# Stage boundaries of a two-block transformer kernel: column halves of the second tokens, GpSimd for first splits and first layer norms, chunk halves for a stage's first two tiles

## The reference

```
for layer in (0, 1):                                   # first block
    h = modulate(rmsnorm(x)); y = mlstm(h) if layer == 0 else stick_breaking(h, k_sh, v_sh)
    x = x + g1 * y
    h = modulate(rmsnorm(x)); x = x + g2 * peer_ffn(h) # 128*128 experts, top 16 of 8 heads
for l in (0, 1):                                       # second block
    mix = diff_moba(x) if l == 0 else gla(x)
    x = layer_norm(alpha * x + mix)
    x = layer_norm(alpha * x + relu(x @ w1)**2 @ w2)   # width 4096
```

## Time and profile before

| | |
|---|---|
| median of three runs | 2693.94 us (2690.03, 2693.94, 2698.76) |
| the profiled execution, span from first to last instruction | 2688.2 us |
| TensorE matmul busy | 2605.5 us, 97% |
| VectorE, ScalarE, GpSimd busy | 1996.2 (74%), 1506.0 (56%), 346.1 us (13%) |
| mean granted clock of TensorE | 0.995 |

### The profile page before, as it was taken

How to read it: one execution, slowest core, us unless ns; L and a number is a source line. 1 busy time by engine, 2 the same in 40 slices (tenths; PEclk the granted TensorE clock), 3 DMA queues, 4 the chain that set the end, 5 groups by cost and what they waited for, 6 DMA issues and landing times.

```text
span 2688.2 us, 48883 instructions
## 1 busy us (share of the span) xinstructions
PE 2605.5 (97%) x17304; PEld 2387.0 (89%) x17304; DVE 1996.2 (74%) x3791; ACT 1506.0 (56%) x2602; POOL 346.1 (13%) x190
## 2 busy tenths in 40 slices
PE   6999999999999999999999999999999999998998
PEld 6779999999888888889999999888888889887997
DVE  6768957888887876669867888666666686677766
ACT  4455557766565556555557766665554544463443
POOL 4007600000000002617500000000000101002000
PEclk9999999999999999999999999999999999999999
DMA  6844564444788874424664444555555345442553
GB/s 243 282 137 164 197 228 149 142 143 148 266 279 272 280 264 145 149 94 167 204 213 143 148 142 150 195 191 192 195 187 187 108 176 188 165 164 96 187 188 133
DMA packets 134733, 490.88 MB, mean 183 GB/s; under 512 B 15520, under 2 KB 15608, under 8 KB 134288
## 3 DMA queue, kind: packets, MB, share of 16 engines
q1 hardware_dynamic: 131904, 480.31, 52.6%
q0 software_dynamic: 2640, 8.02, 0.9%
HBM read 487.21 MB, written 1.06 MB: 182 GB/s over the span
## 4 chain that ended last, share of the span: by engine, by line
PE 87%; DVE 6%; ACT 2%; DMA 2%; issue 1%; POOL 0%; SPq 0%; DVEq 0%; ACTq 0%
PE ps L224 78%; PE ps L1308 4%; DMA weight_ring<-in_stream 2%; ACT weight_split L239 1%; PE ps L641 1%; DVE weight_split L248 1%; DVE arena L633 1%; ACT arena L396 1%; PE ps L2473 1%; PE ps L1280 1%; POOL weight_split L248 0%; DVE arena L1909 0%; PE ps L389 0%; DVE arena L1913 0%; PE ps L662 0%
## 5 line engine op out<-in xcount | busy, mean ns | idle before, releaser
L224 PE MATMUL ps<-hT_split,weight_split 128*128 128x256 f32 x9792 | 1234.3, 285 | 9.8 <-DVE hT_split L421 4.6
L224 PEld LDWEIGHTS ps<-hT_split,weight_split 128*128 128x128 f32 x9792 | 1196.2, 192 | 20.1 <-issue 13.8
L248 DVE TENSOR_TENSOR weight_split<-weight_ring,weight_split 128x1024 fp32r<-128x1024 f32 x674 | 823.5, 1223 | 403.0 <-ACT weight_split L239 400.4
L239 ACT ACTIVATE weight_split<-weight_ring 128x1024 fp32r<-128x1024 f32 x800 | 848.2, 1061 | 259.7 <-PE ps L224 167.8
L224 PE MATMUL ps<-weight_split,hidden_split 128*128 128x512 f32 x3948 | 914.8, 391 | 7.6 <-DVE hidden_split L1574 4.0
L224 PEld LDWEIGHTS ps<-weight_split,hidden_split 128*128 128x128 f32 x3948 | 736.4, 188 | 160.9 <-issue 8.0
L248 POOL TENSOR_TENSOR weight_split<-weight_ring,weight_split 128x1024 fp32r<-128x1024 f32 x126 | 306.2, 2433 | 410.5 <-ACT weight_split L239 410.2
L1404 ACT ACTIVATE hidden_split<-arena 128x256 fp32r<-128x256 f32 (+1 forms) x256 | 176.3, 689 | 249.0 <-PE ps L224 248.5
L1396 ACT ACTIVATE arena<-ps 128x256 f32<-128x256 f32 (+18 forms) x248 | 126.9, 512 | 133.5 <-PE ps L224 133.5
L224 PE MATMUL ps<-weight_split,hT_split 128*128 128x512 f32 x660 | 159.1, 396 | 9.0 <-DVE weight_split L248 4.7
L1574 DVE TENSOR_TENSOR hidden_split<-arena,hidden_split 128x256 fp32r<-128x256 f32 x256 | 161.2, 630 | 0.0
(11 more groups left out here) (357 smaller groups left out, 1765.7 us busy)
## 6 DMA issues: line engine op xcount, KB each, us to landing
weight_ring<-in_stream SPq DMA_DIRECT2D x912, 512.0 KB, 3.3
x<-in_x SPq DMA_DIRECT2D x1, 1024.0 KB, 5.0
arena<-mlstm_m_rows POOLq DMA_DIRECT2D x1, 1024.0 KB, 6.7
arena<-in_ln_mix_g POOLq DMA_DIRECT2D x2, 512.0 KB, 4.8
arena<-in_ln_mix_b POOLq DMA_DIRECT2D x2, 512.0 KB, 6.2
arena<-in_ln_ffn_g POOLq DMA_DIRECT2D x2, 512.0 KB, 4.6
arena<-in_ln_ffn_b POOLq DMA_DIRECT2D x2, 512.0 KB, 6.3
out<-x SPq DMA_DIRECT2D x2, 512.0 KB, 2.6
```

Of the source, the lines that this page charges most:

```text
L224: mm = pe.matmul(out_, stationary(s_part), moving(m_part), start=start and n == 0, stop=stop and n == 2, skip_group_check=True)
L239: act.activation(wsplit[:, n % SPLITS, HIGH, :], ring[:, slot(POS[n]), :], ACT.Copy).then_inc(high_ready, 1)
L248: eng.tensor_tensor(w[:, REST, :], ring[:, slot(POS[n]), :], w[:, HIGH, :].bitcast(fp32), ALU.subtract).then_inc(split_ready, 1)
```

## The change

- **Second tokens by column halves.** A stage's tail runs the held-back matmuls of tb = 1 for columns 0 to 511 first (`third_done`), then for 512 to 1023. Residual, squares, scaling and the layer norm's sum and statistics are done by these halves; transposes g = 2 and g = 3 wait for a half each. `dense_pe` now holds back three tiles instead of two.
- **GpSimd.** The rests of the first two tiles of peer 0, stick breaking, peer 1, mlp0, gla and mlp1, the high of the second tile of the three rms stages, the rest of hy's first tile, and the unit rows of the first tokens (two instructions of 512 columns) of the three layer norms move to GpSimd. The parameter DMAs that followed on GpSimd now stand behind them.
- **Turn.** The chunks 0 to 3 of the second tokens are split on VectorE as two pieces of 2 chunks (5 parts instead of 4); TensorE starts when the first piece is there.
- **First two tiles by chunk halves.** `two_lin_cols`: chunks 0 to 3 of tile 0, then of tile 1, then chunks 4 to 7 of each.
- **Small.** The epsilon goes into the root's bias; `HOLDS` gets other numbers; tile 1 of an mlp uses bank 3.

```diff
-        HOLDS = {1: (28, 2, 4, 14, 2), 2: (28, 5, 4, 14, 0), 4: (28, 5, 4, 14, 0), 6: (0, 1, 26, 14, 1),
-                 7: (0, 7, 26, 14, 0), 8: (0, 6, 26, 14, 0)}
+        HOLDS = {1: (14, 2, 2, 12, 2), 2: (14, 5, 2, 12, 0), 4: (14, 5, 2, 12, 0), 6: (0, 1, 8, 10, 1),
+                 7: (0, 7, 8, 10, 0), 8: (0, 6, 8, 10, 0)}
...
+SPLIT_WAITS = {True: {0: 2, 2: 3, 4: 4, 6: 5}, False: {0: 2, 4: 3, 6: 4}}
...
+        def two_lin_cols(n, dsts, turn):
+            for chunks in (range(4), range(4, 8)):
+                for k, dst in enumerate(dsts):
+                    if chunks[0] == 0:
+                        pe.wait_ge(split_ready, n + k + 1)
+                    w = wsplit[:, (n + k) % SPLITS]
+                    for c in chunks:
+                        if k == 0:
+                            chunk_split(turn, c)
+                        mm = passes(dst, lambda part: w[:, part, c * 128:(c + 1) * 128], lambda part: hTsplit[:, part, c, :], c == 0, c == 7)
+                    if chunks[0]:
+                        mm.then_inc(tiles_used, 1)
...
+        def norm_turn_dve(n, normed):
+            part_split_dve(n, 1, lambda v: half_of(v, 0), normed)
             for m in range(2):
+                part_split_dve(n, 2 + m, lambda v: v[:, 2 * m:2 * m + 2, 128:T], normed)
+            for m in range(2):
+                part_split_dve(n, 4 + m, lambda v: pair_of(v, m), normed)
...
+            def gated_sum(tb, columns, done):
+                y = ps[:, bank + 2 * tb:bank + 2 * tb + 2, :].rearrange("p a b -> p (a b)")
+                after_dve(dve.tensor_tensor(tok[:, tb, columns], y[:, columns], gate[:, columns], ALU.mult))
+                dve.tensor_tensor(x[:, tb, columns], x[:, tb, columns], tok[:, tb, columns], ALU.add).then_inc(done, 1)
...
-            splits_until(dve, n0)
-            rest(dve, n0)
-            rows_done(k, 1, done_tiles)
-            after_dve(gated_dve(1, gate, bank))
+            gated_sum(0, slice(0, D), x_half)
+            dve.wait_ge(third_done, k + 1)
+            gated_sum(1, slice(0, 512), x_third)
+            dve.wait_ge(tiles_used, done_tiles)
+            gated_sum(1, slice(512, D), x_ready)
             if rms is not None:
+                rms_bias_dve(rms)
                 rms_tok_dve(rms, 0)
                 rms_tok_dve(rms, 1)
...
+        def layer_norm_dve(k, done_tiles, bank=0):
+            dve.wait_ge(half_done, 4 + k + 1)
+            after_dve(ln_sum_dve(0, slice(0, D), bank))
+            after_dve(ln_half_stats_dve(0, 0), ln_half_stats_dve(0, 1))
+            ln_var_dve(0)
+            dve.wait_ge(third_done, 4 + k + 1)
+            after_dve(ln_sum_dve(1, slice(0, 512), bank))
+            ln_rstd_dve(k, 0).then_inc(ln_rstd, 1)
+            ln_half_stats_dve(1, 0)
+            dve.wait_ge(tiles_used, done_tiles)
+            after_dve(ln_sum_dve(1, slice(512, D), bank))
+            after_dve(ln_half_stats_dve(1, 1))
+            ln_var_dve(1)
+            after_dve(ln_rstd_dve(k, 1))
+            ln_unit(dve, 1, 0).then_inc(unit_third, 1)
+            ln_unit(dve, 1, 1).then_inc(x_ready, 1)
+
+        def layer_norm_pool(k, n0):
+            pool.wait_ge(ln_rstd, k + 1)
+            ln_unit(pool, 0, 0).then_inc(unit_first, 1)
+            ln_unit(pool, 0, 1).then_inc(x_half, 1)
+            splits_until(pool, n0)
+            rest(pool, n0)
+            rest(pool, n0 + 1)
...
+        def first_rests_pool(n0):
+            splits_until(pool, n0)
+            rest(pool, n0)
+            pool.wait_ge(tiles_used, n0 + 1 - SPLITS + 1)
+            pool.wait_ge(tile_full[slot(POS[n0 + 1])], full(POS[n0 + 1]))
+            pool.tensor_copy(wsplit[:, (n0 + 1) % SPLITS, HIGH, :], ring[:, slot(POS[n0 + 1]), :]).then_inc(high_ready, 1)
+            rest(pool, n0 + 1)
...
+            down(*first, 0, False, False, 0)
+            down(*second, 0, False, False, 0)
+            down(*third, 0, False, True, 0).then_inc(half_done, 1)
+            down(*first, 0, False, False, 1)
+            down(*second, 0, False, False, 1, (0,))
+            down(*third, 0, False, True, 1, (0,)).then_inc(third_done, 1)
+            down(*second, 0, False, False, 1, (1,))
+            down(*third, 0, False, True, 1, (1,))
...
         def peer_pool(l):
+            first_rests_pool(FIRST[f"peer{l}q"])
             pool.wait_ge(x_ready, 2 * l + 1)
             pool.dma_start(pr_sk, io["sub_keys"][l]).then_inc(pr_par, 16)
...
         def hy_params_pool():
+            splits_until(pool, HY_T)
+            rest(pool, HY_T)
```

More of the change, by code:

```diff
@@ L257, in chunk_split, with tile @@
         def chunk_split(turn, c):
-            if turn is not None and c in (0, 4, 6):
-                pe.wait_ge(x_split_ready, 4 * SPLIT_TURNS.index(turn) + {0: 2, 4: 3, 6: 4}[c])
+            if turn is not None:
+                waits = SPLIT_WAITS[OUT_PARTS[turn] == 5]
+                if c in waits:
+                    pe.wait_ge(x_split_ready, SPLIT_BASE[turn] + waits[c])
         def lin_rows(n0, bank, turn=None, tail=False, split=None, split0=0, between=None, rows_of=lambda part, c: hTsplit[:, part, c, :]):
-            def tile(c, tb):
+            def tile(c, tb, halves=(0, 1)):
                 if tb in (None, 0):
@@ L268, in tile @@
                 for b in range(TB) if tb is None else (tb,):
-                    for half in range(2):
+                    for half in halves:
                         mm = passes(ps[:, bank + 2 * b + half, :], lambda part: rows_of(part, c)[:, b * 128:(b + 1) * 128],
@@ L287, in lin_rows @@
                 mm.then_inc(half_done, 1)
-                for c in range(8 - SPLITS, 8):
-                    tile(c, 1).then_inc(tiles_used, 1)
+                tile(5, 1).then_inc(tiles_used, 1)
+                tile(6, 1, (0,))
+                tile(7, 1, (0,)).then_inc(third_done, 1)
+                tile(6, 1, (1,)).then_inc(tiles_used, 1)
+                tile(7, 1, (1,)).then_inc(tiles_used, 1)
         def lin_cols(n, dst, i=0, step=1, turn=None, moving=hTsplit):
@@ L697, in down @@
                 for b in range(TB) if tb is None else (tb,):
-                    for half in range(2):
+                    for half in halves:
                         mm = passes(ps[:, 2 * b + half, :], lambda part: hidden[:, j % 3, part, b * 128:(b + 1) * 128],
                                     lambda part: w[:, part, half * 512:(half + 1) * 512], start, stop)
-                if tb != 0:
+                if tb != 0 and 1 in halves:
                     mm.then_inc(tiles_used, 1)
@@ L1072, in mlstm_dve @@
                 if a == 3:
-                    for tb in range(TB):
-                        rms_var_dve(0, tb)
                     rms_tok_dve(0, 0)
```

304 lines of the change are left out of this document (151 added, 153 removed).

## The result

The changed kernel took 2703.95 us, the median of six runs (2700.89 to 2704.5); the kernel before, over six runs, 2690.34 us (2686.84 to 2698.76). The ratio is 1.0046, 95% interval 1.0033 to 1.0060: slower, by 9 to 16 us. The forecast time, 2700.9 us, was 3 us from it, partly by luck: the sum of the parts was +7.0 us and the measured difference is +12.4 by the ratio (0.0046 x 2690.34). The three runs from which I started had 2693.94 as their median; the three later ones (2686.84 to 2690.65) lay lower, and this made up for part of the sum's error.

A forecast was written before the change was run, and what follows sets the result against it. TensorE was 87% of the chain that ended last, so the change works on seven boundaries and the end. Terms 6.0 + 0.8 + 1.4 - 0.9 + 0.4 - 0.65 = +7.0 us on 2693.9 gave 2700.9 us, range 2680 to 2710.

The forecast's parts named there:

- three rms boundaries and the stages behind them: Peer 0, stick breaking, peer 1: held VectorE +1.45, early splits -0.38, clock +0.9 each; +6.0 us for three.
- mlp0: Layer-norm boundary: start +0.25, early splits -0.38, clock +0.9; +0.8 us.
- gla, from mlp0's tail to its first products: Layer-norm boundary: start, gate weight's rest, longer tail, late chunks and clock; +1.4 us.
- mlp1: Layer-norm boundary: VectorE late as before, shorter chain shows, -0.7 - 0.38 + 0.2 for the clock; -0.9 us.
- hy: Boundary where only the first tile's rest moves: its add is held like peer 0's, without a copy; +0.4 us.
- end, without mlp1's first products: Kernel's end: three held-back tiles gain 1.4 us, 0.6 to 0.75 lost waiting for the last hidden rest; -0.65 us.
- Taking turns: VectorE and GpSimd at the boundaries wait for each other's whole instructions; the forecast itself, 72%, 2694 to 2709 us.
- the clock's part: TensorE's clock falls after over 4 us without work at rms boundaries; 0.9 us each, bounds 0 and 2.3.
- The overlap rival: GpSimd's instructions do not hold VectorE's at the boundaries: -17 us, 2677 us; 18%.
- Dear GpSimd: One-input GpSimd instructions (copy, unit rows) cost what two-input ones do: +7, 2708 us; 10%.
- Chunk halves and end: Early splits save 0.38 us between a stage's first two tiles; three held-back tiles at the end give -0.65 us.

The follow-up runs named there:

- more_holds: The changed kernel with 44 instead of 14 identity transposes ahead of the turn at the three rms boundaries: 2698.5 us, ratio 1.0023.
- no_gpsimd_work: The changed kernel with all of its new GpSimd work undone, halves kept: 2682.99 us, ratio 0.9974 to the kernel before.
- units_back: The changed kernel with only the layer norms' unit rows of the first tokens back on VectorE: 2699.31 us, ratio 1.0029.
- before_two_rests_gpsimd: The kernel before, with GpSimd making the rests of the first two tiles at the three rms boundaries: 2696.27 us, ratio 1.0026.
- hy_rest_back: The changed kernel with only the rest of hy's first tile back on VectorE: 2698.92 us, ratio 1.0022.
- norm_rests_back: The changed kernel with the first two tiles' rests of mlp0, gla and mlp1 back on VectorE, unit rows still on GpSimd: 2699.29 us, ratio 1.003.

## Why the prediction was right or wrong

| term | predicted | measured in the trace |
|---|---|---|
| three rms boundaries and the stages behind them | +6.0 | +6.3 - 0.9 = +5.4 |
| mlp0 | +0.8 | +1.73 - 0.33 = +1.4 |
| gla, from mlp0's tail to its first products | +1.4 | +0.95 + 0.36 + 0.69 = +2.0 |
| mlp1 | -0.9 | +0.68 - 0.32 = +0.4 |
| hy | +0.4 | +0.33 + 2.65 + 1.56 = +4.5 |
| end, without mlp1's first products | -0.65 | -0.73 + 0.32 = -0.4 |
| mLSTM, no edit of the boundary yet | 0 | +0.92 |

- **Taking turns: right in kind and place at the rms boundaries.** The hold of the third quarter's add and of the scaling, the clock below 1 and a start 10.5 to 11.3 us behind the last row product (forecast: 10 and the clock's part) came as put down; the order of turns was the forecast one at all three boundaries. The start, predicted at 194.2 + 0.9 in before's clock, came at 196.18 - 0.92 = 195.26. In sizes: the hold is +1.0 (more_holds) where I had +1.45, the clock +0.7 to +1.8 where I had 0.9. The Trainium skill (SBUF — State Buffer, "Who interferes with whom") says which VectorE instructions are held, and the trace agrees for GpSimd's rests: adds and scalings held (2.12 instead of 0.69, 2.78 instead of 0.88 us), the product from PSUM not.
- **The overlap rival: refuted** as a behaviour, but its arithmetic was that of another kernel. It gave -1.8 to -2.4 a boundary if nothing were held; no_gpsimd_work has 2.05, 1.05 and 2.05 us less than before, because GpSimd makes no split there that could hold VectorE; at stick breaking the parameter work still does.
- **Dear GpSimd: half right, and only for the unit rows.** The copy took 1.50 in all 15 cases of five traces, but each time it began 0.6 us before the held add ended, so no run shows what it takes alone: from the add's end on it is 0.90, and my 1.2 lies between the two. The unit rows took 2.07, outside my bounds of 0.5 and 1.2: I had bounded an operation with no row by a two-input one of the same engine, as if inputs set its time. At mlp1 this is 0.9 us (units_back) of the 1.3 by which the term missed (-0.9 forecast, +0.4 measured). From VectorE's first sum to the start it is 13.21 us before, 13.94 after, 13.00 with the unit rows back and 11.30 with no new work on GpSimd. The 13.21 holds a fall of the clock: in before_two_rests_gpsimd, the same kernel there, the clock stayed up, 26 holds took 3.00 instead of 4.67 and it was 12.31.
- **hy: the step that failed.** I wrote "only the rest moves: its add is held like peer 0's" and priced the hold alone. The hold left TensorE idle for 2.03 instead of 1.70 us, the clock fell, and 72 matmuls behind it paid 2.65. hy_rest_back gives back 1.13 of the gap and 2.16 of the product, so this much is the edit's own. I had given the clock a term at five boundaries and not at the one whose long product follows at once. The fall came in all six kernels with 2.03 us there and in neither of the two with 1.70. The 1.56 at 2140 happens with and without the edits, and its cause stays open.
- **Chunk halves and end: right in the main.** 6.30 became 5.99 at the two peers (forecast -0.38). At stick breaking the first two tiles didn't stand one behind the other before, 16 transposes lay between them, so nothing stood to be won: three tiles with these transposes took 10.6 us before and after. The rest of the -0.9 in the table are other parts of the three stages. Three held-back tiles gave -0.4 in the table's row, with the 0.69 of waiting as forecast.
- **The sum** was +7.0 against +12.4. The rows of the table add up to the 14.2 us between the two traces; 4.1 of the distance to +7.0 is hy, of which the 1.56 came by chance in this trace, and 1.3 mlp1.

Single traces can't be subtracted to better than some microseconds here. The end of mLSTM's rows lay between 182.13 and 186.25 us in twelve kernels whose code up to there is the same but for small statistics; the granted clock of the first 160 us was 0.94 to 0.97. So gaps were compared in traces and totals by medians.

## What to carry to other kernels

Before work is moved to an idle GpSimd, list what VectorE must do in the same microseconds: each of its instructions with two SBUF inputs, and each scaling or cast, may wait for a whole GpSimd instruction, and a hold of 1.4 us that leaves TensorE idle can cost its clock and, as at hy here, 1.3 to 2.6 us more in the product behind it. A gap between two stages tells what a boundary costs only where the last product itself sets its pace; where another engine comes late, as at mlp1, count from that engine's first instruction. The part of such a change that shortens a chain (here column halves, two tiles at a time and three held-back tiles: -7 us, and -12 with three rests placed better) is worth running without the part that offloads. Here a wait for the transposes had room for a VectorE split, at half of GpSimd's price (1.22 against 2.39 us).

## What the runs showed of the hardware that was not expected

The one that waits does not always go next. In the kernel before, at mlp0, GpSimd zeroes four buffers in a row:

```profile
2207.88 3.65 POOL L2416 MEMSET arena<- 128x1024 f32 x4
2208.08 3.60 DVE L767 CAST hidden_split<-arena 128x256 fp32r<-128x256 f32 x1
```

A cast of 256 columns that takes 0.29 us elsewhere took 3.60 (3.79 in the changed kernel): it waited for all four, not for one. So the alternation by single instructions that the prediction was built on is what splits and copies show here, not what every GpSimd instruction does; why the zeroing keeps its turn is open.

GpSimd's unit row did not hold VectorE. In norm_rests_back, at mlp0 (the first line is both halves of the first tokens on GpSimd, the last is what TensorE starts behind the second):

```profile
2160.24 4.15 POOL L579 TENSOR_SCALAR x<-x,stat 128x512 f32<-128x512 f32 x2 [5.55 <-DVE stat L575]
...
2162.84 1.00 DVE L579 TENSOR_SCALAR x<-x,stat 128x512 f32<-128x512 f32 x2
...
2163.76 1.22 DVE L256 TENSOR_TENSOR weight_split<-weight_ring,weight_split 128x1024 fp32r<-128x1024 f32 x1
...
2164.44 1.11 PE L415 MATMUL ps<-ident,x 128*128 128x128 f32 x4 [1.41 <-POOL x L579]
```

VectorE's two unit halves take 1.00 together, as they do without GpSimd beside them, and the rest at 2163.76, with two SBUF inputs, its usual 1.22, while GpSimd's instruction runs to 2164.39, and that one isn't lengthened either (2.06 to 2.08 in every trace). The Trainium skill (SBUF — State Buffer, "Who interferes with whom") says that an instruction with two SBUF inputs contends with a GpSimd instruction that reads SBUF; this one reads SBUF and did not contend, though its overlap with the rest is only 0.6 us, here as at gla and mlp1. GpSimd's subtraction (two inputs) and its copy did: adds beside them ended 0.55 us behind GpSimd's end. Per element this unit row is the slowest of GpSimd's splits, copies and zeroings in these traces, 2.07 us for 512 columns with one input, where a subtraction of 1024 columns with two takes 2.38.
